# Hybrid decoder layer: the opening reordered, with modulation weights for one, one, then two feature blocks at a time

## The reference, cut to what matters

```python
mod = jax.nn.silu(c) @ w_ada[l] + b_ada[l]            # c: 1024, w_ada: 1024 x 6144
sh1, sc1, gt1, sh2, sc2, gt2 = [m[:, None, :] for m in jnp.split(mod, N_MOD, axis=-1)]
h = rms_norm(x, g_norm_mix[l]) * (1.0 + sc1) + sh1
proj = h @ w_in[l]                                    # 1024 x 8704; q, f, i, g, attention q, k, v, two gates
```

## Time and profile before

| | us |
|---|---|
| time of the kernel, median of 3 runs | 951.63 |
| the profiled execution's own time | 952.29 |
| its span, first to last instruction | 950.6 |
| PE busy in the span | 915.2 |
| first product of unit 0 | 25.31 |
| first product of unit 2 (the opening is over) | 53.81 |

### The profile page before, as it was taken

How to read it: one execution, slowest core, us unless ns; L and a number is a source line. 1 busy time by engine, 2 the same in 40 slices (tenths; PEclk the granted TensorE clock), 3 DMA queues, 4 the chain that set the end, 5 groups by cost and what they waited for, 6 DMA issues and landing times.

```text
span 950.6 us, 11767 instructions
## 1 busy us (share of the span) xinstructions
PE 915.2 (96%) x4487; PEld 771.1 (81%) x4487; DVE 441.2 (46%) x707; ACT 363.2 (38%) x482; POOL 439.2 (46%) x390
## 2 busy tenths in 40 slices
PE   2999999998999999999999999999999999999996
PEld 1788888987888888888888888888888888888885
DVE  4843467765456979976723526232222222200005
ACT  4433425242344223453323326555444544412113
POOL 2588433443243344345544445644544445444554
PEclk9999999999999999999999999999999999999998
DMA  9832221212143758443435131322223322233212
GB/s 316 264 132 89 89 89 45 89 45 89 45 142 132 225 175 287 147 133 123 189 104 214 60 132 45 128 95 88 88 88 99 120 89 88 88 122 100 89 44 89
DMA packets 93767, 114.47 MB, mean 120 GB/s; under 512 B 2158, under 2 KB 84250, under 8 KB 93726
## 3 DMA queue, kind: packets, MB, share of 16 engines
q1 hardware_dynamic: 93726, 113.89, 36.1%
HBM read 111.76 MB, written 2.12 MB: 120 GB/s over the span
## 4 chain that ended last, share of the span: by engine, by line
PE 44%; issue 30%; POOL 19%; DVE 3%; ACT 1%; DMA 1%; POOLq 0%; SPq 0%; DVEq 0%; ACTq 0%
PE bank L1051 44%; POOL w_lo L656 18%; DVE bank L1514 1%; DMA x_in<-in_x_dram 1%; DVE bank L1988 0%; DVE x L1989 0%; PE bank L1054 0%; DVE xn_ffn L1885 0%; ACT h_tmp L762 0%; POOL masks L593 0%; ACT w_hi L735 0%; POOL masks L630 0%; DVE h_tmp2a L1570 0%; DVE part L1516 0%; DVE bank L1512 0%
## 5 line engine op out<-in xcount | busy, mean ns | idle before, releaser
L656 POOL TENSOR_TENSOR w_lo<-w_raw,w_hi 128x512 fp32r<-128x512 f32 x292 | 387.3, 1357 | 457.5 <-ACT w_hi L735 452.5
L1051 PE MATMUL bank<-h_hi,w_hi 128*128 128x512 f32 (+1 forms) x880 | 340.3, 390 | 0.1
L1051 PE MATMUL bank<-h_lo,w_hi 128*128 128x512 f32 (+1 forms) x880 | 336.7, 386 | 0.0
L1051 PE MATMUL bank<-h_hi,w_lo 128*128 128x512 f32 (+1 forms) x880 | 261.1, 385 | 0.0
L735 ACT ACTIVATE w_hi<-w_raw 128x2048 fp32r<-128x2048 f32 x72 | 137.5, 1910 | 223.2 <-PE bank L1051 223.2
L1051 PEld LDWEIGHTS bank<-h_hi,w_lo 128*128 128x128 f32 x880 | 165.6, 188 | 33.2
L1051 PEld LDWEIGHTS bank<-h_lo,w_hi 128*128 128x128 f32 x880 | 165.4, 188 | 32.8
L1051 PEld LDWEIGHTS bank<-h_hi,w_hi 128*128 128x128 f32 x880 | 165.1, 188 | 32.8 <-POOL h_lo L643 0.3
L1051 PE MATMUL bank<-w_hi,act_hi 128*128 128x512 f32 x176 | 68.5, 389 | 0.0
L1051 PE MATMUL bank<-w_lo,act_hi 128*128 128x512 f32 x176 | 68.5, 389 | 0.0
L1051 PE MATMUL bank<-w_hi,act_lo 128*128 128x512 f32 x176 | 68.5, 389 | 0.0
(11 more groups left out here) (250 smaller groups left out, 1133.6 us busy)
## 6 DMA issues: line engine op xcount, KB each, us to landing
w_raw<-in_w_in_dram SPq DMA_DIRECT2D x32, 1024.0 KB, 5.2
w_raw<-in_w_up_dram SPq DMA_DIRECT2D x22, 1024.0 KB, 5.0
ada<-in_w_ada_dram SPq DMA_DIRECT2D x16, 1024.0 KB, 5.3
w_raw<-in_w_down_dram SPq DMA_DIRECT2D x11, 1024.0 KB, 4.8
ada<-in_w_ada_dram SPq DMA_DIRECT2D x16, 512.0 KB, 8.4
w_raw<-in_w_out_dram SPq DMA_DIRECT2D x4, 1024.0 KB, 5.1
x_in<-in_x_dram SPq DMA_DIRECT2D x4, 512.0 KB, 5.4
w_raw<-in_w_in_dram SPq DMA_DIRECT2D x8, 256.0 KB, 7.2
```

What stands on the lines that cost most here:

```text
L656: ins = pool.tensor_tensor(wlo[slot][:, cols], raw[slot][:, cols], whi[slot][:, cols].bitcast(F32), ALU.subtract)
L1051: return pe.matmul(o, lhsT, rhs, start=start, stop=stop, **kw)
```

## The change

The part of feature blocks becomes a group g: groups 0 and 1 are one block each, groups 2 to 4 two blocks each. Their transfers are cut in quarters. The small vectors move from SP's queue to ACT's. The shares have a semaphore for each unit. The roots are made one row tile at a time, DVE scales row tiles 0 to 2 and ACT tile 3. `modulated(g)` stands directly behind `group_sums(g)`. In ACT's program `first_h` comes ahead of `high_share` for j = 1 to 3. PE's order is written out block by block, with the passes apart. The diff, cut to its core:

```diff
+MOD_GROUPS = ((0,), (1,), (2, 3), (4, 5), (6, 7))
@@ SP
+            def ada_quarter(g, q):
+                ks = slice(2 * q, 2 * q + 2)
+                k0, n = MOD_GROUPS[g][0], len(MOD_GROUPS[g]) * P
+                for i in range(2):
+                    sp.dma_start(group_columns(g)[:, ks, n * i:n * i + n],
+                                 cols_of(w_ada, D * i + P * k0, n)[:, ks, :]).then_inc(ada_in[g][q], 16)
-            for half in range(2):
-                ada_half(0, half)
-            rows(vec_rows, B_ADA, b_ada.rearrange("l (k p) -> (l k) p", p=P), 48)
...
+            for g in range(len(MOD_GROUPS)):
+                for q in range(4):
+                    ada_quarter(g, q)
+                if g != 1:
+                    first_shares(max(g - 1, 0))
+            ready(sp, ("mod1", 2))
@@ POOL
-            pool.wait_ge(sq_done, TT)
-            inverse_root(0, TT)
+            for t in range(TT):
+                pool.wait_ge(sq_done, t + 1)
+                link(pool.tensor_scalar(rstd[:, t:t + 1], ssq[:, t:t + 1], 1.0 / D, EPS, ALU.mult, ALU.add))
+                pool.tensor_tensor(rstd[:, t:t + 1], rstd[:, t:t + 1], mhalf[:, 0:1], ALU.pow).then_inc(first_root, 1)
             for j in range(KT // 2):
+                if j < KT // 2 - 1:
+                    low_h(2 * j)
+                    if j:
+                        low_h(2 * j + 1)
                 low_share(j, 0)
                 low_share(j, 1)
-                if 0 < j < KT // 2 - 1:
-                    low_h(2 * j)
-                if j < KT // 2 - 1:
-                    low_h(2 * j + 1)
+                if j == 0:
+                    low_h(1)
@@ ACT (the seven transfers of the small vectors now stand here, ahead of everything else)
             for j in range(KT // 2):
-                act.wait_ge(share_in[j], 16 * 2)
-                high_share(j, 0)
+                if j == 0:
+                    high_share(j, 0)
+                first_h(2 * j)
+                if j:
+                    first_h(2 * j + 1)
+                    high_share(j, 0)
                 high_share(j, 1)
-                first_h(j)
                 if j == 0:
+                    first_h(1)
@@ PE
+            def growing_products(u, k, w, a):
...
+                    pe.wait_ge(h_hi_done, k + 1)
+                    if j < KT // 2 - 1:
+                        pe.wait_ge(hi_share, 2 * j + u + 1)
+                    else:
+                        pe.wait_ge(hi_done, u + 1)
...
+            first_modulation(2)
+            for g in (2, 3):
+                for k in MOD_GROUPS[g]:
+                    for u in range(2):
+                        growing_products(u, k, *high)
+                for k in MOD_GROUPS[g + 1]:
+                    transposed_x(k)
+                for k in MOD_GROUPS[g]:
+                    for u in range(2):
+                        growing_products(u, k, *h_low)
+                first_modulation(g + 1)
+                for u in range(2):
+                    for k in MOD_GROUPS[g]:
+                        growing_products(u, k, *w_low)
+            for u in range(2):
+                for what in (high, h_low, w_low):
+                    for k in MOD_GROUPS[-1]:
+                        growing_products(u, k, *what)
@@ DVE
-                    if j == 1 and k == 1:
-                        low_h(0)
-                    if j > 1 and k == 1:
-                        modulated(j - 1)
+            scaled_x(0)
+            b = ready(dve, "vec")
...
+            for t in range(1, TT - 1):
+                scaled_x(t)
+            for g in range(len(MOD_GROUPS)):
+                group_sums(g)
+                modulated(g)
```

More of the change, by code:

```diff
@@ L120, in plan_banks @@
         use(("xT", 0, k), "start")
-    for j in range(KT // 2):
-        use(("mod1", j), "mod1")
+    for g in range(len(MOD_GROUPS)):
+        use(("mod1", g), "mod1")
     for u, t, pool in ((0, 0, "gemm"), (0, 1, "gemm"), (1, 0, "gemm"), (1, 1, "fourth")):
@@ L345, in layer_kernel @@
         hi_done = sem("hi_done")
-        share_in = [sem(f"share_in{j}") for j in range(KT // 2)]
+        share_in = [[sem(f"share_in{j}_{u}") for u in range(2)] for j in range(KT // 2)]
         hi_share, lo_share = sem("hi_share"), sem("lo_share")
@@ L353, in layer_kernel @@
         c_in, vec_in = sem("c_in"), sem("vec_in")
-        ada_in = [[sem(f"ada_in{j}_{half}") for half in range(2)] for j in range(KT // 2)]
+        ada_in = [[sem(f"ada_in{g}_{q}") for q in range(4)] for g in range(len(MOD_GROUPS))]
+        first_root = sem("first_root")
         pair_done = sem("ada_pair_summed")
@@ L370, in layer_kernel @@
         rstd_done = sem("rstd_done")
-        xn_done = [sem("xn_act"), sem("xn_dve")]
+        xn_done = [sem(f"xn_done{t}") for t in range(TT)]
         xn2_done = [sem(f"xn_ffn_tile{t}") for t in range(TT)]
@@ L483, in _ @@
         def _(sp):
-            def rows(dst, r0, src, n):
-                sp.dma_start(dst[r0:r0 + n, :], src).then_inc(vec_in, 16)
             def load_unit(u, src, slot):
@@ L1092, in transposed_x, with first_transposes @@
                 filled(ins, ("xT", 0, k))
+            def first_transposes():
+                bb = [claim(pe, ("xT", 0, k)) for k in range(2)]
+                for t in range(TT):
+                    pe.wait_ge(xn_done[t], 1)
+                    for k in range(2):
+                        ins = transpose(bb[k][:, t * P:(t + 1) * P], xn_in[:, t, k * P:(k + 1) * P])
+                        if t == TT - 1:
+                            filled(ins, ("xT", 0, k))
             def unit_parts(u, slot, width):
@@ L1522, in modulated @@
[L1522 to L1529 removed]
+                        stt(part[:, g % 2, 0:n], src, sc, acc, ALU.mult, ALU.add).then_inc(pair_done, 1)
@@ new lines, in modulated @@
+            def modulated(g):
+                b = ready(dve, ("mod1", g))
+                k0, n = MOD_GROUPS[g][0], len(MOD_GROUPS[g])
+                cols, scales = slice(k0, k0 + n), slice(KT + k0, KT + k0 + n)
+                tt(mod[:, cols], b[:, 0:n], vec[:, B_ADA + k0:B_ADA + k0 + n], ALU.add)
+                release(tt(mod[:, scales], b[:, n:2 * n], vec[:, B_ADA + KT + k0:B_ADA + KT + k0 + n], ALU.add), ("mod1", g))
+                evacuated(dve, ("mod1", g))
+                stt(a1[:, cols], mod[:, scales], 1.0, vec[:, G_MIX + k0:G_MIX + k0 + n], ALU.add,
```

213 lines of the change are left out of this document (97 added, 116 removed).

## The result

The changed kernel takes 963.10 us (median of four runs, 963.01 to 963.96); the kernel before took 952.25 us beside it (four runs, 951.01 to 952.90). The ratio is 1.0118, with a 95% interval of 1.010 to 1.0135. So it is 10.85 us slower, where 5.9 us were forecast (957.5 against 951.63), and it lies 2.1 us above the range. The profiled execution took 963.01 us, with a span of 961.3 us.

What follows compares the result with a forecast made beforehand. TensorE bounds the kernel, so only unit 2's start counts: 59.6 instead of 53.8 us, +5.8. 952.29 + 5.8 = 958.1, less 0.66 to the median, 957.4, plus a tenth for restarts: 957.5 us; range 954.0 to 961.0.

Steps and rivals of the forecast that it cites:

- free for modulation 2: Opening, group 2: TensorE, from modulation 1's end at 22.6, does products and transposes and is free at 30.1 us.
- 0.52 us for a sum instruction of 256 columns: DVE's sums of single blocks: 0.52 us an instruction, 4.2 for eight, between bounds of 0.48 and 0.79.
- Half clock: Opening, behind the 3.8 us idle ahead of block 2: TensorE's work grows by up to 2 us, 959.4; chance 0.27.
- likeliest case: The forecast of 957.5 us, with unit 2 at 59.6 us and no fall of TensorE's clock; chance 0.48.
- So nothing further is lost: End of opening: POOL has unit 2's split ready at 61.9, TensorE wants it at 67.0, the same distance as before.
- No change: Rival: in the opening DVE's chain paces alone, TensorE and ACT answer at once; unit 2 at 54.2, 952.0 us; chance 0.08.
- faster: Rival: in the opening replies to DVE are hidden too; unit 2 3.8 us earlier, 947.8 us; chance 0.05.
- Small transfers: Rival: 128 KB pieces of groups 0 and 1 come slowly, holding up sums(1) 1.5 us, 959.0; late or slow transfers 0.12.
- bound of half the rate: Loads of groups 0 and 1: at half of 349 GB/s, 2.1 MB take 6 us more, group 1 complete at about 22.
- 15 us for these 2.1 MB: Loads of groups 0 and 1: estimate at the skill page's 138 GB/s, 15 us instead of 6, time about 962.
- The issues: SP's queue in the opening: 16 issues at 0.33 us each, 5.3 us, are no bound.
- as the bound allowed: Head: small vectors on ACT's queue may land at 11 us instead of about 6, costing DVE up to 1.4 us.

Runs made afterwards that it cites:

- e4: Changed kernel plus products of zeros on TensorE in two of its idles (four behind modulation 2, two behind the low-weight pass of blocks 2 and 3): 958.95 us.
- e5: Changed kernel with the rounding (cast) of unit 2's weights moved from DVE to ACT, behind ACT's last shares: 963.49 us.
- e1: Changed kernel with ACT rounding both shares ahead of h again for j = 1 to 3, as before the change: 957.64 us.
- e7: Kernel before, with ACT making h of both blocks ahead of rounding the shares for j = 1 to 3: 963.07 us.
- e12: e1 plus two products of zeros on TensorE ahead of the high pass of block 2: 956.64 us.
- e6: e3 plus modulations 2 to 4 taken earlier on TensorE and the small vectors read behind the first sums: 952.55 us.
- e3: Changed kernel with ACT's shares ahead of h and DVE's scale inside the next sum, both as before the change: 956.53 us.
- e9: Kernel before with the new head alone (roots by row tile, DVE scales tiles 0 to 2, small vectors on ACT's queue): 951.80 us.
- e8: Kernel before with DVE's scale of a pair of blocks directly behind its sum, not inside the next sum: 953.37 us.
- e2: Changed kernel with DVE's scale inside the next sum, behind its second instruction, as before the change: 960.93 us.
- e10: e6 plus one product of zeros on TensorE ahead of the high pass of block 2: 950.95 us.

## Why the prediction was right or wrong

**Where it was right.** The direction, the place and the cause. The schedule that was worked out stands in the trace within 0.3 us wherever the clock is full:

| step | forecast | measured |
|---|---|---|
| first sum, first product | 11.6, 18.8 to 19 | 11.85, 19.11 |
| free for modulation 2 | 30.1 | 30.09 |
| idle ahead of blocks 2, 4 | 3.8, 2.0 | 3.93, 1.98 |
| products of block 2 begin | 34.9 | 34.96 |
| from there to modulation 3 | 4.8 | 7.19 |
| modulation 3 to products of block 4 | 4.8 | 4.88 |
| from there to modulation 4 | 4.8 | 6.21 |
| modulation 4 to products of block 6 | 4.8 | 4.88 |
| from there to unit 2 | 5.5 | 6.43 |
| idle of DVE ahead of scales 3, 4 | some 3 | 5.40, 4.43 |
| unit 2 | 59.6 | 64.55 |

The 0.52 us for a sum instruction of 256 columns, which no row of before had, came out: seven of them begin from 11.85 to 15.52 us. That 30.1 is met so closely is partly luck: the eight transposes took 0.79 us instead of 1.0, which hides that the four products ahead of them took 1.16 instead of 0.9.

**The step that failed: "Half clock".** Its working said that the idle ahead of block 2 might bring it, for up to 2 us, once, and left it out of the likeliest case because 3.8 us is shorter than the 4.43 us of the earlier trace rows. It came twice, for 2.5 and 1.5 us (e4). The first was under-sized because I took from the earlier trace rows that the clock is back after 2 us; here it was at 0.50 from 35 to 40 us, over all eight products and all the transposes (1.56 us instead of 0.79 in e4). The second was not in any case: I took the nearest row for a bound. Behind its opening the trace of before had one more idle over 1 us, of 1.53 us, with the clock at 1.00 behind it, and nothing between the two. So it says that the clock falls at 4.43 us, and not where it starts to; nor does it have an idle of this length among light work. The range should have held two such falls, 957.5 + 4.0 = 961.5 us, and even this would not have been enough without the next step.

**The second step that failed: "So nothing further is lost".** I had compared POOL's weights for unit 2 with the time at which TensorE wants them, and that was right. But TensorE also wants a bank that DVE frees with `hq`, and this chain had no slack even before: `hq` began at 53.03 and unit 2 0.78 us behind it, at 53.81, exactly where TensorE's own work ended; after the change, where the bank is what ends the wait, it is 63.77 and 64.55, 0.78 us again. The changed order puts POOL's low shares beside the cast ahead of `hq`, and with no slack all of it comes through: 0.9 us (e5).

**The sum.** 5.8 + 2.5 + 1.5 + 0.9 = 10.7 us, as measured; unlike in the forecast, the two half clocks and the bank are now terms with rows. For the profiled executions it closes: 952.29 + 10.7 = 963.0, measured 963.01. The forecast of the median lies lower still, since it took off 0.66 us by which the profiled execution of before lay above its median; with a fourth run that median is 952.25, and the changed kernel's profiled execution lies at its median.

**The parts.** ACT's order is the largest: undone, it gives back 6.2 us (e1), and put alone into the kernel before it costs 10.7 (e7), by waits of its own. With it undone, 4.6 us remain. Of these 1.9 go when one idle is filled (e12). All go with e6, and a little more, but e6 undoes DVE's order, takes the modulations earlier and reads the small vectors later at once, and only the first of these was run without the others (e3). That TensorE's late answers are the rest is argued, not shown. The head's 1.6 us stand in the profiles (e9), but the first sum of before was the latest of the three kernels with the old head, and the time doesn't tell it from nothing. DVE's order costs 1.7 us by the schedule in the kernel before (e8), and less in the changed one (e2), where DVE had time to spare; with ACT's order undone it is 1.56 us ahead of block 6 (e3).

**The rivals.** "No change" and "faster" fell for the reason that was held against them, the programs' order. "Small transfers" fell as a rival: DVE's sums of groups 1 and 2 began without a wait for data. But they are not free, as these windows of the changed kernel, and of the kernel before below, show:

```profile
10.00:12.00 2.00, 0.94 (x5) 0.30 (x3) 1.89 (x6) 1.15 (x2) 1.78 (x3) 1.00 1.18 311
...
16.00:18.00 2.00, 0.98 (x4) 0.93 (x4) 0.80 (x5) 0.38 (x1) 0.00 (x0) 1.00 1.17 310
```

```profile
10.00:12.00 2.00, 0.00 (x0) 0.00 (x0) 0.00 (x0) 1.15 (x2) 0.37 (x2) 1.00 1.10 360
...
16.00:18.00 2.00, 1.83 (x9) 1.83 (x10) 1.93 (x3) 0.12 (x2) 0.00 (x0) 1.00 1.07 354
```

Over 8 to 18 us the mean is 311 GB/s instead of 347, so 0.36 MB or 1.0 us of data come later. In e9, which has the new head and the old pieces, it is 352. Here DVE was late anyway; in e6 and e10 it may be a part of what DVE's last sums wait for, which no run tested. My bound of half the rate was far too low a rate, and so was the estimate from the Trainium skill ("DMA: Bandwidth & Descriptors", section Bandwidth, Measured), 15 us for these 2.1 MB: at 311 GB/s they take 6.8. Its figure is for transfers issued from GpSimd, and these came from SP.

The issues were under-sized too: the first eight on SP took 6.45 us, 0.81 each, and not 0.33. They are not dear for being small: in the kernel before, the first four, of 512 KB each, took 4.98 us, 1.25 each. The rows, after and before:

```profile
3.10 6.45 SPq L511 DMA_DIRECT2D ada<-in_w_ada_dram  x8
```

```profile
3.10 4.98 SPq L506 DMA_DIRECT2D ada<-in_w_ada_dram  x4
```

The small vectors landed late, as the bound allowed: DVE's copy of them began at 9.86 us; the first sum came 0.25 us later than forecast.

## What to carry to other kernels

When a change makes the engine that sets the time stand still, price its lower clock with every idle of 1.5 us and more that stands among light work, as a term that can come several times, and try a product of zeros in its place: it told the two causes apart here and was worth 0.4 to 4 us. Where an engine makes two inputs of the same step, put the one whose data are there already first, so that only the late one is waited for. And follow all that the next stage needs, its banks as well as its weights, before writing that nothing further is lost.

## What the runs showed of the hardware

- TensorE was granted 0.50, its 1.2 GHz level, behind the idle ahead of block 2 wherever it was left open (3.93 to 4.00 us in three kernels, 2.06, 1.99 and 1.47 us in e3, e1 and e6) and ahead of block 4 (1.98, 2.04 and 1.96 us in the changed kernel, e2 and e5), but not behind the single one ahead of block 6 (1.96 to 1.98 us in four kernels), nor behind 2.31 us in e7. Behind 1.19 + 0.60 us it was in e3 and not in e1. Behind 1.52 to 1.53 us in the middle of steady products it stayed at 1.00 in 14 of 14 profiles. So the length of the idle alone doesn't decide; what does was not isolated. The Trainium skill ("TensorE: Matmul & The Clock Gate", section "A second HAM failure mode: psum-queue depth-cycling") tells of a clock that goes back and forth when TensorE often stands still for short times between groups of products; the rows agree, with two falls and two rises between 33 and 51 us in the changed kernel.
- Early in the opening the granted clock doesn't show all: in the changed kernel it reads 1.00 from 22.5 to 27.5 us, while the eight products of 512 columns from 22.65 to 26.21 us came 0.45 us apart, and 0.23 a little later.
- Products of zeros, added to a bank in use, kept the granted clock at 1.00 through the same stretch (e4, e10, e12).
- A cast of 128 x 2048 numbers on DVE took 1.84 us instead of 1.22, and an instruction of four columns 1.25 instead of 0.16, beside POOL's work with two inputs; POOL's took 3.52 instead of 2.52.
- While pieces of 128 KB with rows of 512 bytes came in, the DMA moved 311 GB/s instead of 347 for pieces of 512 KB (352 in e9). Whether the size of the pieces or their rows is the reason was not told apart.
